# Long convolution on Trainium2: half of the direct spectrum products moves from VectorE to GpSimd

## The reference, cut to what matters

```python
def long_conv(u, spec, skip):
    L = u.shape[1]
    uf = u.astype(F32)
    y = jnp.fft.irfft(jnp.fft.rfft(uf, n=2 * L, axis=1) * spec, n=2 * L, axis=1)[:, :L]
    return (y + uf * skip.astype(F32)).astype(u.dtype)

def hyena_mixer(u, conv_w, spec, skip):
    u = short_conv(u, conv_w)
    v, x1, x2 = jnp.split(u, 3, axis=-1)
    z = x1 * long_conv(v, spec[:, 0], skip[0])
    return x2 * long_conv(z, spec[:, 1], skip[1])
```

## Time and profile before

| | us |
|---|---|
| median of 3 runs | 3372.62 |
| lowest and highest | 3366.08, 3375.44 |
| the profiled execution, its own time | 3373.11 |
| its span in the trace | 3371.3 |
| mean granted clock of TensorE | 0.995 |

### The profile page before, as it was taken

How to read it: one execution, slowest core, us unless ns; L and a number is a source line. 1 busy time by engine, 2 the same in 40 slices (tenths; PEclk the granted TensorE clock), 3 DMA queues, 4 the chain that set the end, 5 groups by cost and what they waited for, 6 DMA issues and landing times.

```text
span 3371.3 us, 40184 instructions
## 1 busy us (share of the span) xinstructions
PE 3293.0 (98%) x15296; PEld 2573.6 (76%) x15296; DVE 1591.8 (47%) x2656; ACT 1290.3 (38%) x1953; POOL 1586.9 (47%) x1234
## 2 busy tenths in 40 slices
PE   8999999999999999999899999999999999999999
PEld 7787777788778767667777888876766777778887
DVE  4566434547444788535543321247864555342020
ACT  4343643333453322544445322232254444443231
POOL 4554345555434553234463555655322435537473
PEclk9999999999999999999999999999999999999999
DMA  4323225332223423222442433342331235334332
GB/s 152 97 88 91 85 88 160 97 100 85 88 75 114 166 76 125 66 72 78 139 156 66 147 104 104 104 137 85 115 92 57 76 110 166 102 115 129 97 94 94
DMA packets 127112, 353.12 MB, mean 105 GB/s; under 512 B 16574, under 2 KB 16894, under 8 KB 126920
## 3 DMA queue, kind: packets, MB, share of 16 engines
q1 hardware_dynamic: 126920, 350.55, 33.3%
HBM read 315.89 MB, written 25.17 MB: 101 GB/s over the span
## 4 chain that ended last, share of the span: by engine, by line
PE 86%; DVE 6%; POOL 3%; issue 2%; ACT 2%; DMA 1%; SPq 0%; DVEq 0%; ACTq 0%; POOLq 0%
PE B L881 25%; PE B L883 24%; PE B L882 24%; PE B L925 2%; POOL WSP L1582 1%; PE B L1015 1%; PE B L1042 1%; PE B L1111 1%; PE B L1204 1%; DMA WRAW<-in_wb 1%; PE B L1092 1%; PE B L986 1%; PE B L977 1%; POOL FACC L1630 1%; DVE B L1671 1%
## 5 line engine op out<-in xcount | busy, mean ns | idle before, releaser
L1582 POOL TENSOR_TENSOR WSP<-WRAW,WSP 128x512 fp32r<-128x512 f32 x1038 | 1364.1, 1336 | 1568.2 <-ACT WSP L1237 1567.7
L881 PE MATMUL B<-H,WSP 128*128 128x512 f32 x2496 | 995.8, 399 | 17.1 <-DVE H L1755 9.3
L883 PE MATMUL B<-H,WSP 128*128 128x512 f32 x2496 | 973.2, 390 | 0.0
L882 PE MATMUL B<-H,WSP 128*128 128x512 f32 x2496 | 972.6, 390 | 0.0
L1237 ACT ACTIVATE WSP<-WRAW 128x1024 fp32r<-128x1024 f32 (+1 forms) x568 | 556.2, 984 | 693.9 <-PE B L883 533.3
L881 PEld LDWEIGHTS B<-H,WSP 128*128 128x128 f32 x2496 | 469.1, 188 | 142.9 <-issue 25.3
L882 PEld LDWEIGHTS B<-H,WSP 128*128 128x128 f32 x2496 | 469.5, 188 | 101.3 <-issue 7.4
L883 PEld LDWEIGHTS B<-H,WSP 128*128 128x128 f32 x2496 | 468.9, 188 | 99.4
L1671 DVE TENSOR_TENSOR B<-B,RN 128x512 f32<-128x512 f32 x194 | 135.1, 697 | 449.9 <-PE B L883 446.9
L881 PE MATMUL B<-YM,WSP 128*128 128x512 f32 x512 | 199.4, 389 | 0.0
L883 PE MATMUL B<-YM,WSP 128*128 128x512 f32 x512 | 199.2, 389 | 0.0
(11 more groups left out here) (425 smaller groups left out, 4825.4 us busy)
## 6 DMA issues: line engine op xcount, KB each, us to landing
WRAW<-in_wb SPq DMA_DIRECT2D x318, 512.0 KB, 3.7
WRAW<-in_wa SPq DMA_DIRECT2D x154, 512.0 KB, 3.8
WRAW<-in_wa SPq DMA_DIRECT2D x48, 256.0 KB, 2.6
WRAW<-in_wb SPq DMA_DIRECT2D x48, 256.0 KB, 2.7
parked<-HYT SPq DMA_DIRECT2D x24, 256.0 KB, 2.1
QA<-RXA SPq DMA_DIRECT2D x64, 64.0 KB, 2.0
xs<-PA SPq DMA_DIRECT2D x16, 256.0 KB, 4.6
WIN<-in_win SPq DMA_DIRECT2D x16, 256.0 KB, 3.1
```

The lines of the kernel that those rows point to most:

```text
L881: e.matmul(o, L[0], R[0], start=first, stop=False)
L882: e.matmul(o, L[0], R[1], start=False, stop=False)
L883: return e.matmul(o, L[1], R[0], start=False, stop=last)
L1582: x = e.tensor_tensor(WSP[:, i % NSP, 1, c:c + CUT], WRAW[:, i % NRAW, c:c + CUT], WSP[:, i % NSP, 0, c:c + CUT].bitcast(fp32), ALU.subtract)
```

## The change

For j2 = 0 the six operations of `uprod` go from DVE's program into POOL's, at the same unit of the list, in both transforms of both layers. They write the same tiles in the same order. `ysplit` for j2 = 0 now waits for POOL's results of the direct product and, as before, for DVE's of the mirrored one. The products for j2 = 1 stay on DVE.

```diff
@@ gpsimd
+                elif k == "uprod" and a[2] == 0:
+                    l, o, j2 = a
+                    X, F = spectrum("uspec", o, j2), spectrum("fspec", o, j2)
+                    t1, t2 = terms(j2)[:2]
+                    w.wait_ge(dve_done, ("whole", 1, "uspec", *a))
+                    e.tensor_tensor(t1, X[0], F[0], ALU.mult).then_inc(*pool_done.up(("p0", *a)))
+                    e.tensor_tensor(t2, X[2], F[2], ALU.mult).then_inc(*pool_done.up(("p1", *a)))
+                    w.wait_ge(pool_done, ("p0", *a))
+                    e.tensor_tensor(F[0], X[2], F[0], ALU.mult).then_inc(*pool_done.up(("p2", *a)))
+                    w.wait_ge(pool_done, ("p1", *a))
+                    e.tensor_tensor(F[2], X[0], F[2], ALU.mult).then_inc(*pool_done.up(("p3", *a)))
+                    e.tensor_tensor(t1, t1, t2, ALU.subtract).then_inc(*pool_done.up(("re0", *a)))
+                    w.wait_ge(pool_done, ("p3", *a))
+                    e.tensor_tensor(F[2], F[2], F[0], ALU.add).then_inc(*pool_done.up(("im0", *a)))
@@ vector, uprod
                     l, o, j2 = a
+                    if j2 == 0:
+                        continue
@@ vector, ysplit
-                        w.wait_ge(dve_done, (ready + "0", *a))
+                        w.wait_ge(dve_done if j2 else pool_done, (ready + "0", *a))
```

## The result

The changed kernel took 3381.23 us (median of 8 runs, 3378.13 to 3383.11), the kernel before 3371.62 beside it (8 runs, 3366.08 to 3376.62). The ratio is 1.0028, 95% interval 1.0018 to 1.0038: 9.6 us slower, by the interval 6 to 13, and just inside the 0.3% that the prediction set as its bound for "no change". A second measurement of the same kernel gave 3380.63 against 3373.10, ratio 1.0028 (1.0019 to 1.0036). The prediction was 3381, in a range from 3373 to 3388.

The account below looks back on a forecast made before the run. TensorE, busy 98% of the span, was taken to bound the kernel, so only its waits count. Stall and clock in two layers less the o=0 gain, 2 x (3.05 + 2.0) - 1.65 = +8.45 us, gave 3381; range 3373 to 3388.

Parts of the forecast that it names:

- o=1, remainder 223 late: Second transform: POOL makes the remainder of weight 223 after the product, so TensorE stands 3.05 us longer per layer.
- POOL's price: Each moved 128x512 operation takes 1.26 us on POOL, six 7.55 us; the ends are 7.5 and 9.2.
- quiet-neighbour argument: During the new products DVE's work has a bank as an operand, so POOL is not slowed to its dear rows.
- internal waits: Waits between the product's own operations on POOL cost nothing; without an instruction between, an estimated 0.14 us each.
- o=0, weight 218: First transform: freed DVE lets POOL's remainder 218 come earlier, TensorE's wait goes; -0.82 us per layer, -1.65 in all.
- The fold of o=0: First transform: DVE's ysplit, needing POOL's sixth operation at 1241.3, gets there about 1242; no cost.
- The clock: Behind each o=1 stall TensorE's granted clock falls for a while; 2.0 us taken per layer, between 0 and 2.9.
- DVE's idle time before the scaling: Second transform: DVE idle 8 us instead of 4.74 before the scaling near 1299.
- Rival 1: POOL later still at remainder 223 in o=1: products of 8.3 to 9.2 us, 3384 to 3386; chance 0.17.
- rival 2: POOL in time in o=1: only the 1.65 us gain of o=0 is left, 3371; chance 0.08.
- Rival 3: Clock does not fall behind the o=1 stalls: only the stall is paid, +4.5 us, 3377; chance 0.15.

Follow-up runs that it names:

- e2: Kernel before with only the product of the second transform (o=1) of each layer moved to POOL; 3381.82 us, ratio 1.0030.
- e3: Changed kernel, but in o=1 POOL makes remainder 223 (406 in layer 1) before the product; 3371.74 us, ratio 1.0001; again 3372.11, ratio 0.9995.
- e4: Changed kernel with three further multiplies on POOL ahead of the product of o=1, results written over; 3389.75 us, ratio 1.0051.
- e5_real_half: Changed kernel, but in o=1 POOL makes only three of the six operations, DVE the other three; 3371.63 us, ratio 0.9998.

## Why the prediction was right, point by point

- **o=1, remainder 223 late: right.** Predicted 3.05 us a layer, measured 2.90 from start to start (1294.81 to 1297.94, less 0.23), 3.04 with the slower restart (the first matmul behind the wait takes 0.50 us for 0.39). The term had the sign and place that carried the whole result; e2, e3 and e4 show it by removing and enlarging it.
- **POOL's price: right.** 1.26 taken, 1.25 measured. The quiet-neighbour argument held: no operation of the products took over 1.31 us in this profile, and the starts stay 1.25 apart over the internal waits. (Where e5_real_half has such a wait without an instruction between, the next start came 0.13 us later; the prediction's estimate was 0.14.) The Trainium skill's "about 2x slower" for two inputs (GPSIMD Engine Reference, section 4.1, Engine selection) agrees: 1.25 against DVE's 0.60 is 2.1. Its advice against the move was right for this order of the queue and empty for the order of e3_remainder_first, where the slower engine made no loss that 11 runs show (-2.7 to +3.4 us).
- **o=0, weight 218: right in the trace.** -0.82 predicted, -0.93 measured per layer; no median here is sharp enough for the 1.9 us together.
- **The fold of o=0: right.** No wait, with 0.56 us of margin.
- **The clock: mis-sized in place, near in sum.** I took 2.0 behind each wait, 4.0 together. It was 1.6 behind one of the two. Some 3 us of other falls that no step of the prediction had made up for it, so the closeness of 3381.0 to 3381.23 is in part luck: by its stretches the sum would have been 3378.
- **DVE's idle time before the scaling: wrong, at no cost.** I wrote 8 us in place of 4.74. It was 9.41, behind another wait of 3.53. The first is the old 4.74 plus TensorE's whole lateness of 4.66, clock included, where I had added the stall alone. The second is the time of the moved operations: DVE now waits already for the gate before.
- **Rival 1** (a product over 8 us) and **rival 2** (POOL in time) did not occur; rival 2's state is what e3 makes, and its 3371 is near what e3 measured (3371.74; 3372.11 the second time). **Rival 3** (no fall) holds behind 5 of the 10 waits.

## What to carry to other kernels

When work moves to an engine with half its time free, look for the places where it would stand in the queue, and ask at each what is behind it and for when that is due: here the same six operations cost nothing in one place and 3 us of a saturated TensorE in another. What an engine can do early (a remainder whose input has long been there) belongs ahead of what has to wait for its input; swapping the two gave the whole loss back. A late operand has a threshold: up to its margin it is free, beyond it each microsecond counted in full here (3.66 us of wait for 3.67 of delay).

## What the runs showed of the hardware

- DVE operations with two SBUF inputs beside POOL's took up to 1.78 us in place of 0.68 (1.27 where they overlapped for part of the time, in e5_real_half), and POOL's pair 3.0 to 3.5 in place of 2.55; with a bank as one input neither engine slowed (0.68 to 0.70 for DVE beside POOL's product of 1.29 to 1.31 an operation). The Trainium skill (GPSIMD Engine Reference, section 1, Specifications) names this contention; its size is from these traces.
- TensorE idle for 2.74 us in an otherwise dense stretch: the granted clock fell in 5 of 10 cases. Idle for 2.45 us: in 0 of 4. Idle for 6.4 us: in 2 of 2. The length of the wait alone does not decide: at TensorE's wait of 2.60 to 2.62 us for line 1067 (at 1208.5 and 2338.3 in the kernel before) the clock fell in all 26 cases of the 13 profiles. What makes the difference stays open.
- Executions of one kernel differ by up to 10 us without any difference in their work (3366.08 to 3376.62 in the first 8 runs of the kernel before); in its later runs the mean granted clock lies between 0.993 and 0.997, and 0.001 of it is 3.4 us. A change under some 3 us has to be read in the trace, stretch by stretch.
